# Index tables of a top-k ranking in a free PSUM bank, and the sum of squares on GpSimd

## The reference

```python
q = (hf @ w_q).reshape(T, PEER_HEADS, PEER_DKEY)                    # 8 heads of 256
q = (q - mean(q, -1)) * rsqrt(var(q, -1) + LN_EPS)
s1 = einsum('thd,nd->thn', q[..., :half], k1)                       # 128 scores per half
s2 = einsum('thd,nd->thn', q[..., half:], k2)
v1, i1 = top_k(s1, 16)
v2, i2 = top_k(s2, 16)
cand = v1[..., :, None] + v2[..., None, :]                          # 16 x 16 candidates
vs, j = top_k(cand, 16)
e = take_along_axis(i1, j // 16) * 128 + take_along_axis(i2, j % 16)
g = softmax(vs)
act = gelu(einsum('td,tkd->tk', xb, u[e]))                          # 16384 experts, u and v
out = einsum('tk,tkd->td', g * act, v[e])
```

## Time and profile before

| what | value |
|---|---|
| median of 3 runs | 1434.33 us (1433.47 to 1434.75) |
| the profiled execution, its own time | 1434.41 us |
| its span, first to last instruction | 1432.6 us, mean granted clock 0.990 |
| TensorE busy | 1407.3 us, 98% of the span |
| VectorE busy | 1234.1 us, 86% |
| ScalarE busy | 594.4 us, 41% |
| GpSimd busy | 586.7 us, 41% |
| queries, scores and start of the ranking | 196 to 303 us |
| ranking beside expert tiles | 303 to 456 us |

### The profile page before, as it was taken

One profiled execution on the slowest core, in us unless ns is written; L12 is line 12 of the kernel. 1 busy time (PEld: TensorE's weight loads), 2 busy tenths in 40 slices (PEclk: granted clock), 3 DMA queues, 4 the chain that ended last, 5 costly groups with the idle time before them and its releaser, 6 DMA issues.

```text
span 1432.6 us, 20743 instructions
## 1 busy us (share of the span) xinstructions
PE 1407.3 (98%) x7515; PEld 1236.3 (86%) x7515; DVE 1234.1 (86%) x2019; ACT 594.4 (41%) x698; POOL 586.7 (41%) x397
## 2 busy tenths in 40 slices
PE   7999989999999999999999999999999999999998
PEld 6775478899999999998888888888888888888896
DVE  6988979999999999856788888888898888888888
ACT  3561263333334888843333333333333333333332
POOL 0100125549965000001445545454566646664604
PEclk8899999999999999999999999999999999999999
DMA  9924350015465799998999999999999999999961
GB/s 379 332 118 176 147 195 1 1 58 180 149 233 172 262 294 289 293 344 328 377 368 356 367 375 353 371 356 377 356 373 372 352 388 356 386 353 378 358 243 69
DMA packets 159567, 402.35 MB, mean 281 GB/s; under 512 B 11632, under 2 KB 79344, under 8 KB 156432
## 3 DMA queue, kind: packets, MB, share of 16 engines
q1 hardware_dynamic: 120928, 262.17, 51.7%
q0 software_dynamic: 38288, 139.08, 25.6%
q10 hardware_dynamic: 288, 0.29, 0.1%
HBM read 359.56 MB, written 41.94 MB: 280 GB/s over the span
## 4 chain that ended last, share of the span: by engine, by line
PE 73%; DVE 22%; ACT 2%; DMA 2%; issue 1%; SPq 0%; DVEq 0%; ACTq 0%
PE bank L1007 22%; PE bank L1009 22%; PE bank L1008 22%; DVE arena L1626 2%; DVE arena L1618 2%; DMA wbuf<-ada_w_dram 2%; PE bank L1220 2%; PE bank L1222 2%; DVE arena L1623 1%; DVE arena L1615 1%; DVE arena L1667 1%; DVE arena L1620 1%; DVE arena L1668 1%; PE bank L1096 1%; DVE arena L1664 1%
## 5 line engine op out<-in xcount | busy, mean ns | idle before, releaser
L1007 PE MATMUL bank<-h_lo,u_hi 128*128 128x384 f32 (+1 forms) x1260 | 441.0, 350 | 2.1 <-POOL u_lo L622 1.9
L1009 PE MATMUL bank<-h_hi,u_hi 128*128 128x384 f32 (+1 forms) x1260 | 435.4, 346 | 0.0
L1008 PE MATMUL bank<-h_hi,u_lo 128*128 128x384 f32 (+1 forms) x1260 | 434.8, 345 | 0.0
L1009 PE MATMUL bank<-v_hi,w_hi 128*128 128x512 f32 x744 | 290.7, 391 | 0.0
L1008 PE MATMUL bank<-v_hi,w_lo 128*128 128x512 f32 x744 | 290.5, 390 | 0.0
L1007 PE MATMUL bank<-v_lo,w_hi 128*128 128x512 f32 x744 | 289.5, 389 | 0.3 <-DVE w_lo L1764 0.3
L1007 PEld LDWEIGHTS bank<-h_lo,u_hi 128*128 128x128 f32 x1260 | 237.6, 189 | 14.4 <-ACT arena L836 2.2
L1008 PEld LDWEIGHTS bank<-h_hi,u_lo 128*128 128x128 f32 x1260 | 237.7, 189 | 11.0 <-issue 0.5
L893 ACT ACTIVATE v_hi<-v_raw 128x2048 fp32r<-128x2048 f32 x62 | 118.9, 1918 | 305.9 <-PE bank L1009 296.1
L1009 PEld LDWEIGHTS bank<-h_hi,u_hi 128*128 128x128 f32 x1260 | 237.3, 188 | 9.4
L1758 DVE TENSOR_TENSOR v_lo<-v_raw,v_hi 128x2048 fp32r<-128x2048 f32 x62 | 142.6, 2301 | 106.2 <-ACT v_hi L893 104.5
(11 more groups left out here) (253 smaller groups left out, 1827.1 us busy)
## 6 DMA issues: line engine op xcount, KB each, us to landing
u_raw<-ut_dram SPq DMA_DIRECT2D x128, 512.0 KB, 5.9
v_raw<-v_dram SPq DMA_DIRECT2D x64, 1024.0 KB, 7.3
gate_in<-gates_dram SPq DMA_DIRECT2D x64, 384.0 KB, 7.3
wbuf<-ada_w_dram SPq DMA_DIRECT2D x6, 2048.0 KB, 10.9
early_dram<-arena SPq DMA_DIRECT2D x64, 192.0 KB, 2.7
gates_dram<-wbuf SPq DMA_DIRECT2D x12, 1024.0 KB, 6.9
gates_dram<-arena SPq DMA_DIRECT2D x12, 1024.0 KB, 7.6
w_raw<-early_dram SPq DMA_DIRECT2D x64, 192.0 KB, 5.5
```

What stands on the lines that cost most here:

```text
L1007: pe.matmul(out, a_hi, b_lo, start=(k == 0), stop=False)
L1008: pe.matmul(out, a_lo, b_hi, start=False, stop=False)
L1009: return pe.matmul(out, a_hi, b_hi, start=False, stop=(k == n - 1))
```

## The change

Six edits, all between 196 and 456 us of the kernel before.

1. The places of the chosen candidates (`chosen`), the key positions (`pos`), two decoded arrays (`quarter`, `low`) and a copy of the numbers 0..15 (`numbers`) lie in a PSUM bank: bank 7 for heads 0 and 1, SBUF as before for head 2, bank 0 for heads 3 to 7 (`TABLE_BANKS`). So in the decoding, in the comparisons and in the products one operand comes from PSUM and at most one from SBUF.
2. The copy of the numbers is made once for each bank, after `s_qev` 4 (head 0) or 15 (head 3).
3. The conversion of the positions to float32 (line 1644) and the copy of the chosen values (line 1653) are left out; the product reads the integers, and `top_k` writes its values straight to `vs`.
4. GpSimd adds the two halves of the squared queries in place (`sum_squares`, 128 by 512), after the weights' low parts of the next head, the last one after the second expert tile's split; it waits for `s_qev`.
5. TensorE makes 8 instead of 16 matmuls at line 1155 for each head, after a new wait for `s_sqsum`.
6. TensorE waits for `s_e1e2` 2 (the ranking of heads 0 and 1 done) before it writes the first expert tile to bank 7.

```diff
@@ -104,6 +104,7 @@
 PARTS = len(STORE_PARTS)
 assert sum(PICKS_AT[:PER * AT_GELU]) == PICKS and sum(PICKS_AT) == 2 * PICKS
 BANKS_RANK = (7, 1)
+TABLE_BANKS = (7, 7, None, 0, 0, 0, 0, 0)
 BANKS_SCATTER = (7, 6)
 LAST_BANK_PARTS = (slice(0, D // 4), slice(D // 4, D // 2))
 LAST_BANKS = tuple(zip(LAST_BANK_PARTS, (OUTS - 1, BANKS_SCATTER[1])))
@@ -241,10 +242,10 @@
         third = v_hi.rearrange("p r s d -> p (r s d)")[:, 0:2 * D].rearrange("p (w k n) -> p w k n", w=2, k=KD)
         part = arena[:, ARENA - 2 * CHUNK_C:].rearrange("p (b n) -> p b n", b=2)
 
-        (qT, sq, keys, e1, e2, wt, vs, s_all, s_val, s_pos, s_posf, cand, c_val, c_idx, dec, eq_a, eq_b,
+        (qT, sq, keys, e1, e2, wt, vs, s_all, s_val, s_pos, cand, c_idx, dec, eq_a, eq_b,
          pk) = carve(
             [(2, 2, S), (2, 2, S), (2, NK), (TB, PICKS), (TB, PICKS), (TB, PICKS), (TB, PICKS),
-             (3, TB, DK), (2, TB, K), (2, TB, K), (2, TB, K), (TB, CAND), (TB, K), (TB, K), (8, TB * K),
+             (3, TB, DK), (2, TB, K), (2, TB, K), (TB, CAND), (TB, K), (8, TB * K),
              (TB * K, K), (TB * K, K), (4, TB * H)])
 
         s_of = ([s_all[:, 0], s_all[:, 1], arena[:, ARENA - TB * DK:].rearrange("p (t n) -> p t n", t=TB), s_all[:, 2]]
@@ -320,6 +321,7 @@
             sem(n) for n in ("expert_summed", "expert_gelu", "expert_weighted", "value_summed", "value_added",
                              "picked_zeroed", "final_sd_ready", "final_times_gain"))
         s_fin = [sem(f"output{n}_ready") for n in range(TB)]
+        s_sqsum = sem("query_squares_summed")
         s_wthi, s_wtlo = sem("weights_hi_ready"), sem("weights_lo_ready")
         s_onehot = sem("index_onehots_ready")
         s_first = sem("first_weights_landed")
@@ -607,6 +609,11 @@
 
             pool.dma_start(keys[:, 0, :], k1t).then_inc(s_keys, 16)
             pool.dma_start(keys[:, 1, :], k2t).then_inc(s_keys, 16)
+            def sum_squares(h):
+
+                pool.wait_ge(s_qev, 2 * h + 2)
+                pool.tensor_tensor(sq[:, h % 2, 0], sq[:, h % 2, 0], sq[:, h % 2, 1], ALU.add).then_inc(s_sqsum, 1)
+
             for h in range(1, H):
                 if h == 4:
                     pool.wait_ge(s_centre, 4)
@@ -615,6 +622,7 @@
                 if h > 1:
                     lo_weights(NZ + 2 * h)
                 lo_weights(NZ + 2 * h + 1)
+                sum_squares(h - 1)
 
             def split_u(i, c):
                 pool.wait_ge(s_uhi, i * RT + (c + 1))
@@ -624,6 +632,7 @@
 
             split_u(0, 0)
             split_u(0, 1)
+            sum_squares(H - 1)
             pool.wait_ge(s_wtlo, NZ + 2 * H)
             for n in range(4 * TB):
                 split_u(0, GT + n)
@@ -1150,10 +1159,10 @@
                         at = (tb % 2) * DK + half * NK
                         pe.matmul(bank[(2, 5)[par] + tb // 2][:, at:at + NK],
                                   qT[:, par, half, tb * P:(tb + 1) * P], keys[:, half, :], start=True, stop=True)
+                pe.wait_ge(s_sqsum, h + 1)
                 for tb in range(TB):
-                    for half in range(2):
-                        mm = pe.matmul(bank[4][:, var_at(tb)], sq[:, par, half, tb * P:(tb + 1) * P], mean_col,
-                                       start=(half == 0), stop=(half == 1))
+                    mm = pe.matmul(bank[4][:, var_at(tb)], sq[:, par, 0, tb * P:(tb + 1) * P], mean_col,
+                                   start=True, stop=True)
                 mm.then_inc(s_smm, 1)
 
             def static_at(h):
@@ -1188,6 +1197,7 @@
 
 
             pe.wait_ge(s_qev, 2 * H)
+            pe.wait_ge(s_e1e2, TABLE_BANKS.count(BANKS_RANK[0]))
             for c in range(RT):
                 if c == GT:
                     scores(1, H - 1, False, static_at(H - 1))
@@ -1626,31 +1636,45 @@
                     last = ve.max_index(idx[:, 8:16], val[:, 8:16], data)
                 return last
 
-            ci = c_idx.rearrange("p t k -> p (t k)").bitcast(U32)
-            dci = [dec[:, n, :].bitcast(U32) for n in range(4)]
-            ka, kb, low = dec[:, 4, :], dec[:, 5, :], dec[:, 6, :]
-            iota16 = iota[:, 0:K].unsqueeze(1).to_broadcast([P, TB * K, K])
+            ka, kb = dec[:, 4, :], dec[:, 5, :]
+            per = TB * K
+            tables_in_sbuf = (c_idx, s_pos, dec[:, 0, :], dec[:, 6, :], iota[:, 0:K])
+
+            def tables_of(b):
+
+                if b is None:
+                    return tables_in_sbuf
+                of = bank[b]
+                return (of[:, 0:per].rearrange("p (t k) -> p t k", t=TB),
+                        of[:, per:3 * per].rearrange("p (a t k) -> p a t k", a=2, t=TB),
+                        of[:, 3 * per:4 * per], of[:, 4 * per:5 * per], of[:, 5 * per:5 * per + K])
 
             step = Chain(ve, s_cl).link
 
             def route(h):
 
+                chosen, pos, quarter, low, numbers = tables_of(TABLE_BANKS[h])
                 ve.wait_ge(s_sev, h * 2 + 2)
-                last = top_k([(s_val[:, half, tb, :], s_pos[:, half, tb, :].bitcast(U32),
+                if TABLE_BANKS[h] not in (None,) + TABLE_BANKS[:h]:
+                    ve.wait_ge(s_qev, 2 * H - 1 if h else 4)
+                    step(ve.tensor_copy(numbers, iota[:, 0:K]))
+                last = top_k([(s_val[:, half, tb, :], pos[:, half, tb, :].bitcast(U32),
                                s_of[h][:, tb, half * NK:(half + 1) * NK])
                               for tb in range(TB) for half in range(2)], step)
                 last.then_inc(s_routed, 1)
                 ve.wait_ge(s_routed, h + 1)
-                ve.tensor_copy(s_posf, s_pos.bitcast(U32))
                 ve.tensor_tensor(cand[:, :, 0:CAND_A].rearrange("p t (a b) -> p t a b", a=4),
                                  s_val[:, 0, :, 0:4].unsqueeze(3).to_broadcast([P, TB, 4, K]),
                                  s_val[:, 1, :, :].unsqueeze(2).to_broadcast([P, TB, 4, K]), ALU.add)
                 step(ve.tensor_tensor(cand[:, :, CAND_A:].rearrange("p t (a b) -> p t a b", a=K - 4),
                                       s_val[:, 0, :, 4:].unsqueeze(3).to_broadcast([P, TB, K - 4, 4]),
                                       s_val[:, 1, :, 0:4].unsqueeze(2).to_broadcast([P, TB, K - 4, 4]), ALU.add))
-                step(top_k([(c_val[:, tb, :], c_idx[:, tb, :].bitcast(U32), cand[:, tb, :]) for tb in range(TB)], step))
-
-                ve.tensor_copy(vs[:, :, h * K:(h + 1) * K], c_val)
+                step(top_k([(vs[:, tb, h * K:(h + 1) * K], chosen[:, tb, :].bitcast(U32), cand[:, tb, :])
+                            for tb in range(TB)], step))
+
+                ci = chosen.rearrange("p t k -> p (t k)").bitcast(U32)
+                dci = [quarter.bitcast(U32)] + [dec[:, n, :].bitcast(U32) for n in range(1, 4)]
+                iota16 = numbers.unsqueeze(1).to_broadcast([P, TB * K, K])
                 ve.tensor_scalar(dci[0], ci, 2, None, ALU.logical_shift_right)
                 ve.tensor_scalar(dci[1], ci, 4, None, ALU.logical_shift_right)
                 ve.tensor_scalar(dci[2], ci, 12, None, ALU.bitwise_and)
@@ -1664,8 +1688,8 @@
                 step(ve.tensor_tensor(eq_a, ka.unsqueeze(2).to_broadcast([P, TB * K, K]), iota16, ALU.is_equal))
                 ea = eq_a.rearrange("p (t j) a -> p t j a", t=TB)
                 eb = eq_b.rearrange("p (t j) a -> p t j a", t=TB)
-                ve.tensor_tensor(ea, ea, s_posf[:, 0].unsqueeze(2).to_broadcast([P, TB, K, K]), ALU.mult)
-                step(ve.tensor_tensor(eb, eb, s_posf[:, 1].unsqueeze(2).to_broadcast([P, TB, K, K]), ALU.mult))
+                ve.tensor_tensor(ea, ea, pos[:, 0].bitcast(U32).unsqueeze(2).to_broadcast([P, TB, K, K]), ALU.mult)
+                step(ve.tensor_tensor(eb, eb, pos[:, 1].bitcast(U32).unsqueeze(2).to_broadcast([P, TB, K, K]), ALU.mult))
                 ve.tensor_reduce(e1[:, :, h * K:(h + 1) * K], ea, AX.X, ALU.add)
                 ve.tensor_reduce(e2[:, :, h * K:(h + 1) * K], eb, AX.X, ALU.add).then_inc(s_e1e2, 1)
```

## The result

The changed kernel takes **1420.9 us** (median of 6 runs, 1420.5 to 1421.77) against 1434.3 us (6 runs, 1433.5 to 1434.75) before: ratio 0.9909 [0.9899, 0.9919], 13.4 us faster. I had predicted 1423.7 and a range from 1422.3, so the direction was right and the gain came out 1.4 us beyond the range's lower end.

The account below looks back on a forecast made before the run. The prediction took TensorE to bound the kernel; 5.95 us from the squares' matmuls, 3.74 from the long wait and 0.94 at the turn made 10.6 us, giving 1423.7 us, with a range from 1422.3 to 1429.0.

Parts of the forecast that it names:

- The squares' matmuls: Line 1155 in each head's scores: eight fewer matmuls save 0.85 us a head, none at head 6, together 5.95 us.
- the forecast wait: First expert tile, behind head 6's scores: TensorE waits about 0.9 us for GpSimd's first half of `u_lo`.
- the additions cost nothing: GpSimd's additions of the squares between the queries: 1.25 us each, covered by 3 us left before TensorE needs the low part.
- The long wait: TensorE's 1.88 us wait at 358.92 for a tile's low part, with its clock drop: 3.74 us saved.
- The turn: Nine transposes from 456.47 and the idle time ahead of them: without waits for VectorE and ScalarE, 0.94 us saved.
- The slack at ScalarE's exponentials: Ahead of the turn: shifted values ready at about 415, exponentials at 441, so VectorE has 26 us to spare.
- The sum: Savings of 5.95, 3.74 and 0.94 us make 10.6 us, taking the profiled 1434.41 to 1423.8 and the median to 1423.7.
- One: First expert tile: the new 0.9 us wait lowers TensorE's clock, costing up to 1.9 us; 1425.2 to 1425.6, chance 0.13.
- Two: Near tile 13: a shorter wait for `u_lo` remains; 1424.6 to 1426.5 us, chance 0.13.
- Three: VectorE's rankings: searches into PSUM cost far more and TensorE waits at the turn; 1440 us at 0.28 each, chance 0.03.
- Four: VectorE's rankings: PSUM operands don't end the contention with GpSimd; 1430.6 us, or 1432 with a clock drop, chance 0.07.
- Five: Long stretch of values: the lead is lost again to transfers; 1434 us, chance 0.04.

Follow-up runs that it names:

- the tables alone: The changed kernel with the 16 matmuls of the squares back and no addition on GpSimd, keeping the tables in PSUM: 1427.58 us.
- the repeat: The kernel before run once more with no edit, and profiled again: 1434.35 us.
- the squares alone: The kernel before with only GpSimd's addition of the squares and the 8 fewer matmuls a head, tables still in SBUF: 1446.28 us.
- the last experiment: The changed kernel with early high parts for the first tiles and float16 squares, 8 float16 matmuls a head, no GpSimd additions: 1415.73 us.

## Why the prediction was wrong, by its own steps

**The squares' matmuls: right in kind, 0.35 us too small.** 0.85 us a head was expected; heads are now 13.62 us apart against 14.51, so 0.89. Head 6 gave its saving to the forecast wait (0.98 for 0.9), head 7 gave 0.90 (first tile to turn 148.22 with the tables alone, 147.32 in after). 5.4 + 0.9 = 6.3 us instead of 5.95. That the additions cost nothing holds with the tables in PSUM only.

**The long wait: right in kind.** With a pair of one PSUM and one SBUF operand VectorE no longer stretches (1220 to 1224 ns beside a busy GpSimd), no wait for `u_lo` is left beside the tiles and the 3.74 us came back. I had not looked for its second, smaller sign. In before, ScalarE's `u_hi` starts are 365.06 and 448.91 with 20 tiles between: 83.85 - 20 x 4.16 = 0.65 us lost to another late `u_lo`, near 385 us, which the sum put at nothing. It came back too. But the clock's fall was no fixed part of the price: the repeated kernel had the same 1.88 us at a clock of 1.00 and the same span, with 3.59 us of waiting at the turn instead of 0.39. That the terms read from the one execution came so near the whole is in part luck.

**The turn: mis-sized.** 0.94 us became 0.56 + 0.60, from the end of tile 34's sixth chunk to the transposes and from there through them, and a further 0.27 at the wait ahead of the scatter. That is 1.43 us, 0.49 more. The slack at ScalarE's exponentials was given as 26 us and measured 18.9. A ranking with its tables in PSUM takes 24.96 us in the mean, not 23.8, mostly because the candidate additions still read two SBUF operands and collide; that wasn't on the way to the end.

**The sum: this is the step that failed.** "5.95 + 3.74 + 0.94 = 10.6 us", taken from the profiled execution's own 1434.41. Trace to trace, without the start, it is 5.4 + 6.7 = 12.1. So 1.5 us are terms that were too small or missing: 0.35 of the squares' matmuls, 0.65 of the second late `u_lo`, 0.49 of the turn. For the other 1.3 us of the 13.4 the sum had no term; it took one execution for the kernel. That one had started late (184.74; of the 13 other profiled executions of this study 11 started between 182.85 and 184.23, two at 184.55 and 184.96) and still had the usual time: from start to end it took 1247.84 us, the repeat 1248.85, with longer sixth and seventh rankings ahead of the turn. Against the repeat's stretch the change is worth 13.1 us from start to end, close to the 13.4 of the medians. After the change the rankings have slack and TensorE sets the turn, where a delay costs all of itself. That the kernel before usually loses such a microsecond in its rankings is argued from two executions; eight of its 61 took 2 to 4 us less, so what the 1.3 us are stays open.

**The rivals.** One (the clock falls at the first tile): no, 1.00 from 296 to 443 with a 0.98 us wait. Two (a shorter `u_lo` wait near tile 13): no. Three (dear searches in PSUM): no, 3 to 10 ns. A PSUM source costs the product nothing (1221 ns at the middle against 1224 at best in SBUF); the small integer operation pays 37 ns (232 for 195), and the shortest ranking is 23.84 us against 24.00. The Trainium skill, "VectorE: DVE Perf Modes", in its section on the TRN2 errata, has a dearer fixed cost for a PSUM source, by my estimate from it 65 ns for every such instruction: the product doesn't show it. Four (the contention stays): no. But its price, 1430.6 to 1432 us, left out what the squares do to rankings that still contend: the squares alone took 1446.3. Five (the lead lost to transfers): no, 967.25 us from the scatter to the end against 967.26.

**The range.** Its lower end had head 6's 0.85 us in it and "a little of other waits", and no term for how far the profiled execution may lie from the usual one, although the three runs shown spread over 1.3 us. Its upper end had all the care.

## What to carry to other kernels

Before you add up savings against one profiled execution, profile the kernel a second time: here two executions with the same time came to it by different ways, one later at the start and shorter in its rankings, the other earlier and longer. And ask at each meeting of two engines which one sets the time; what the other gains or loses ahead of it is hidden there. A cheap instruction on GpSimd is only cheap while VectorE's two-input operations beside it read at most one operand from SBUF: the same edit was worth -6.7 us after the tables had moved to PSUM and +12 us ahead of it. For matmuls with one output column the type of the operands was worth more (1.71 to 0.21 us a head) than halving their number (1.71 to 0.82).

## What the runs showed that I had not expected

- The same wait of 1.88 us at the same place brought TensorE's granted clock to 0.50 for some us in one execution and left it at 1.00 in another.
- Identical code comes to the first of the 20 transposes between 182.85 and 184.96 us, by when the clock rises in the first 50 us (0.73 to 1.00 granted from 40 to 50 us).
- A two-input operation of 128 by 256 float32, 0.43 us at the middle in after (line 1666), took 3.84 us with the squares alone, beside a `centre` that began as it did.
- One float32 matmul with a single output column leaves two records of about 0.107 us each, 0.21 us in all; one in float16 leaves a single record, and by the distance to the next instruction's start (0.11 us for 4, in the last experiment 0.21 us for 8) takes 0.03 us.
